# A hybrid attention and mLSTM layer on one core: head pairs on 64 rows each of TensorE, and two output units interleaved

## The reference

```python
# branch a: for each token, 128 keys are chosen by an index score; attention over them
s_idx = einsum('bthd,bsd->bths', qi, ki) * 64 ** -0.5        # 16 index heads of 64
score = einsum('bth,bths->bts', wi, relu(s_idx))             # masked by chunks of 64 tokens
_, idx = top_k(score, 128)
logits = einsum('bthd,btjhd->bthj', q, k[idx]) * 64 ** -0.5  # 8 heads of 64
out = einsum('bthj,btjhd->bthd', softmax(logits), v[idx])
# branch b: mLSTM with 4 heads of 128, gated and normalised by head
# merge
merged = sigmoid(g_a) * ((o_a * silu(a_z)) @ w_branch_a) + sigmoid(g_b) * (h_b @ w_branch_b)
y = rmsnorm(x + merged @ w_out) * final_norm_g
```

## Time and profile before

| | |
|---|---|
| median of 3 runs | 515.43 us |
| the profiled execution | 515.22 us, its span 513.5 us |
| PE matmuls busy | 503.4 us, 98%, 2506 of them |
| PE weight loads busy | 422.1 us, 82% |
| DVE, ACT, POOL busy | 252.1, 236.3, 214.0 us |
| DMA | 48.94 MB, 95 GB/s in the mean |

### The profile page before, as it was taken

How to read it: one execution, slowest core, us unless ns; L and a number is a source line. 1 busy time by engine, 2 the same in 40 slices (tenths; PEclk the granted TensorE clock), 3 DMA queues, 4 the chain that set the end, 5 groups by cost and what they waited for, 6 DMA issues and landing times.

```text
span 513.5 us, 6778 instructions
## 1 busy us (share of the span) xinstructions
PE 503.4 (98%) x2506; PEld 422.1 (82%) x2506; DVE 252.1 (49%) x564; ACT 236.3 (46%) x417; POOL 214.0 (42%) x142
## 2 busy tenths in 40 slices
PE   7999999999999999999999999999999999999995
PEld 7688888888888878788888888888888888887885
DVE  3875778877999915515645556311110011125333
ACT  6756754655534344455567643233321333152322
POOL 1675231333353442356486343056335653372000
PEclk9999999999999999999999999999999999999999
DMA  8744531222233422122213111142244426443112
GB/s 281 207 132 121 142 99 47 83 83 70 63 114 87 139 83 82 42 60 66 82 41 84 42 43 41 42 123 66 60 122 123 110 57 202 124 155 133 41 48 77
DMA packets 44841, 48.94 MB, mean 95 GB/s; under 512 B 4996, under 2 KB 29700, under 8 KB 44808
## 3 DMA queue, kind: packets, MB, share of 16 engines
q1 hardware_dynamic: 43944, 47.39, 31.4%
q10 hardware_dynamic: 864, 1.12, 0.6%
HBM read 46.40 MB, written 2.11 MB: 94 GB/s over the span
## 4 chain that ended last, share of the span: by engine, by line
PE 91%; DMA 3%; POOL 3%; issue 1%; ACT 1%; SPq 1%; DVE 0%; POOLq 0%; DVEq 0%; ACTq 0%
PE pj L1397 23%; PE pj L1398 22%; PE pj L1399 22%; PE ob L1504 3%; DMA w_raw<-in_w_in 2%; POOL w_lo L510 2%; PE tr L1498 2%; PE ob L1478 2%; PE qb L1468 2%; PE qb L1463 2%; PE qb L1462 2%; PE ob L1398 1%; PE qb L1398 1%; PE qb L1397 1%; PE ob L1397 1%; PE ob L1399 1%
## 5 line engine op out<-in xcount | busy, mean ns | idle before, releaser
L510 POOL TENSOR_TENSOR w_lo<-w_raw,w_hi 128x1024 fp32r<-128x1024 f32 x70 | 168.3, 2415 | 147.1 <-ACT w_hi L851 147.0
L1397 PE MATMUL pj<-w_hi,h_hi 128*128 128x512 f32 x272 | 112.8, 415 | 0.0
L1399 PE MATMUL pj<-w_hi,h_lo 128*128 128x512 f32 x272 | 106.5, 392 | 0.0
L1398 PE MATMUL pj<-w_lo,h_hi 128*128 128x512 f32 x272 | 106.5, 392 | 0.0
L1397 PE MATMUL pj<-h_hi,w_hi 128*128 128x512 f32 (+1 forms) x200 | 78.1, 390 | 1.0 <-DVE h_lo L1076 1.0
L851 ACT ACTIVATE w_hi<-w_raw 128x1024 fp32r<-128x1024 f32 (+1 forms) x72 | 73.5, 1045 | 9.6 <-DMA w_raw<-in_w_out 6.0
L1399 PE MATMUL pj<-h_hi,w_lo 128*128 128x512 f32 (+1 forms) x200 | 77.9, 389 | 0.0
L1398 PE MATMUL pj<-h_lo,w_hi 128*128 128x512 f32 (+1 forms) x200 | 77.9, 389 | 0.0
L1399 PEld LDWEIGHTS pj<-w_hi,h_lo 128*128 128x128 f32 x272 | 51.1, 188 | 11.4
L1397 PEld LDWEIGHTS pj<-w_hi,h_hi 128*128 128x128 f32 x272 | 51.2, 188 | 9.5 <-issue 1.0
L1398 PEld LDWEIGHTS pj<-w_lo,h_hi 128*128 128x128 f32 x272 | 51.3, 189 | 9.3 <-issue 1.0
(11 more groups left out here) (200 smaller groups left out, 828.8 us busy)
## 6 DMA issues: line engine op xcount, KB each, us to landing
w_raw<-in_w_in SPq DMA_DIRECT2D x60, 512.0 KB, 3.6
w_raw<-in_w_out SPq DMA_DIRECT2D x5, 512.0 KB, 3.6
x_tok<-in_x SPq DMA_DIRECT2D x4, 512.0 KB, 5.4
w_raw<-in_w_branch_a SPq DMA_DIRECT2D x8, 256.0 KB, 2.9
w_raw<-in_w_branch_b SPq DMA_DIRECT2D x8, 256.0 KB, 3.3
x_again<-in_x SPq DMA_DIRECT2D x1, 2048.0 KB, 9.0
w_late<-in_w_out SPq DMA_DIRECT2D x3, 512.0 KB, 7.2
neg_m_all<-neg_m_d SPq DMA_DIRECT2D x4, 256.0 KB, 5.0
```

The source lines that it names most:

```text
L510: eng.tensor_tensor(lo[:, 0:m], raw_slot(n)[:, 0:m], hi[:, 0:m].bitcast(F32), ALU.subtract).then_inc(lo_by_dve if n in DVE_SLOTS else lo_b ...
L1397: pe.matmul(bank, a_hi, b_hi, start=first, stop=False)
L1398: pe.matmul(bank, a_hi, b_lo, start=False, stop=False)
L1399: return pe.matmul(bank, a_lo, b_hi, start=False, stop=last)
```

## The change

Scores and logits are jobs of two heads each, `score` with 24 jobs instead of 48 and `qk_a` with 16 instead of 32. Head e of a pair has its features on rows 64e to 64e + 63, its queries and keys both, hi and lo in tiles of their own (`iq_parts[:, 0]` hi, `[:, 1]` lo; `k_parts` alike; `q_hi` and `q_lo` instead of `q_twice` and `q_lo`). Its three products go through `tile_position=(64 * e, 0)`, the two heads in turn, head e into bank `qb[e]`. A pair of scores stands where its first head stood; the pair of logits at the even places, while the softmax of one head (`soft`, a job that PE skips) stays at every place. A pair's job takes both banks of the ring. The splits of a whole unit are one copy and one subtraction over 128 rows. The first two output units run seven of their eight chunks each, then the last chunk of each. Of the last scaling ACT has 384 columns and DVE 640 (`SHARE`). Scores and logits are the three products hi by hi, hi by lo and lo by hi; before, the scores' two passes gave the fourth, lo by lo, as well.

```diff
-    for s in range(len(SCORES)):
-        put(score_place(s), "score", s)
+    for k in range(len(SCORES) // 2):
+        put(score_place(2 * k), "score", k)
...
         if p < len(ATTN):
-            put(q, "qk_a", p)
+            if p % 2 == 0:
+                put(q, "qk_a", p // 2)
+            put(q, "soft", p)
...
+        if job[0] in ("score", "qk_a"):
+            assert n[ring] % 2 == 0
+            before[job] = last.get((ring, 1))
+            last[(ring, 0)] = last[(ring, 1)] = job
+            continue
...
             elif kind == "score":
-                eng.wait_ge(relu_made, job[1] + 1)
+                eng.wait_ge(relu_made, 2 * job[1] + 2)
...
             elif kind == "qk_a":
-                eng.wait_ge(z_made, job[1] + 1)
+                eng.wait_ge(z_made, 2 * job[1] + 2)
...
-                    for e in range(2):
-                        src, hi, _ = part(job, e)
-                        act.activation(hi, src, ACT.Copy).then_inc(part_hi_made, 1)
+                    src, hi, _ = part(job)
+                    act.activation(hi, src, ACT.Copy).then_inc(part_hi_made, 1)
...
-                for e in range(2):
-                    same = slice(e * A_DIM, (e + 1) * A_DIM)
-                    act.activation(q_twice[same, i % 2, e, :, :], q_a[same, :, i * P:(i + 1) * P], ACT.Copy)\
-                        .then_inc(q_hi_made, 1)
-                for e in range(2):
-                    same, other = slice(e * A_DIM, (e + 1) * A_DIM), slice((1 - e) * A_DIM, (2 - e) * A_DIM)
-                    act.activation(q_twice[other, i % 2, e, :, :], q_a[same, :, i * P:(i + 1) * P], ACT.Copy)\
-                        .then_inc(q_doubled, 1)
+                act.activation(q_hi[:, i % 2, :, :], q_a[:, :, i * P:(i + 1) * P], ACT.Copy).then_inc(q_hi_made, 1)
...
-                    queries = iq_parts[:, h % 2, h // 2, (i - 1) * P:i * P]
-                    pe.matmul(bank[:, 0:w], queries, ik_hi[:, 0:w], start=True, stop=False)
-                    ins = pe.matmul(bank[:, 0:w], queries, ik_lo[:, 0:w], start=False, stop=True)
+                    for n, (part_q, keys) in enumerate(((0, ik_hi), (0, ik_lo), (1, ik_hi))):
+                        for e in range(2):
+                            same = slice(e * IDX_DIM, (e + 1) * IDX_DIM)
+                            ins = pe.matmul(bank[e][:, 0:w], iq_parts[same, part_q, h // 2, (i - 1) * P:i * P],
+                                            keys[same, 0:w], start=(n == 0), stop=(n == 2),
+                                            tile_position=(e * IDX_DIM, 0))
...
+                    for n, (part_q, part_k) in enumerate(((q_hi, 0), (q_hi, 1), (q_lo, 0))):
+                        for e in range(2):
+                            same = slice(e * A_DIM, (e + 1) * A_DIM)
+                            ins = pe.matmul(bank[e][:, 0:w], part_q[same, i % 2, b, :], k_parts[same, part_k, b, 0:w],
+                                            start=(n == 0), stop=(n == 2), tile_position=(e * A_DIM, 0))
...
-                    half = y_norm[:, i % 2, WIDTH:D_MODEL]
+                    half = y_norm[:, i % 2, SHARE:D_MODEL]
...
-            for m, (i, piece, cols) in enumerate(OUT_UNITS):
...
+            def out_part(m, ks):
...
+            for m in range(2):
+                out_part(m, range(KT - 1))
+            for m in range(2):
+                out_part(m, range(KT - 1, KT))
+            for m in range(2, len(OUT_UNITS)):
+                out_part(m, range(KT))
```

More of the change, by code:

```diff
@@ L726, in side @@
             def side(p):
-                if p == first_quarter("bo"):
-                    wait_full(pool, ("qk_b", B_HEADS - 1, TILES - 1))
-                    pool.wait_ge(lo_by_pool, sum(1 for m in range(group_slot("bz") + 1) if m not in DVE_SLOTS))
-                    for e in range(2):
-                        other = slice((1 - e) * A_DIM, (2 - e) * A_DIM)
-                        pool.memset(q_lo[other, :, e, :, :].bitcast(F32), 0.0).then_inc(q_lo_zeroed, 1)
-                        pool.wait_ge(q_lo_zeroed, e + 1)
                 if p in SPLIT_AT:
                     i = SPLIT_AT[p]
-                    for e in range(2):
-                        same = slice(e * A_DIM, (e + 1) * A_DIM)
[L739 to L743, removed]
+                    pool.wait_ge(q_hi_made, i + 1)
+                    pool.tensor_tensor(q_lo[:, i % 2, :, :], q_a[:, :, i * P:(i + 1) * P],
+                                       q_hi[:, i % 2, :, :].bitcast(F32), ALU.subtract).then_inc(q_lo_made, 1)
                 for job in SIDE.get(p, []):
@@ L796, in _ @@
                 if (g, j) == ("bq", 0):
-                    wait_full(pool, ("score", len(SCORES) - 1))
+                    wait_full(pool, ("score", len(SCORES) // 2 - 1))
                     pool.memset(v_b[:, :, :, B_DIM:B_DIM + 1], 1.0).then_inc(v_ones_made, 1)
@@ L886, in job_side @@
                     wait_full(act, job)
[L887 to L889 removed]
+                    src, hi, _ = part(job)
+                    act.activation(hi, src, ACT.Copy).then_inc(part_hi_made, 1)
                 elif kind == "score":
[L891 to L893 removed]
                     wait_full(act, job)
[L895 to L898, removed]
+                    for s in (2 * job[1], 2 * job[1] + 1):
+                        w = (SCORES[s][0] + 1) * P
+                        if s >= RELUS:
+                            act.wait_ge(relu_used, s - RELUS + 1)
+                        act.activation(ob[s % RELUS][:, 0:w], qb[s % 2][:, 0:w], ACT.Relu,
+                                       scale=float(IDX_DIM) ** -0.5).then_inc(relu_made, 1)
                 elif kind == "qk_b":
@@ L913, in job_side @@
                         .then_inc(cell_made, 1)
-                elif kind == "qk_a":
+                elif kind == "soft":
                     s = job[1]
@@ L1049, in _ @@
                     act.wait_ge(y_gained, m + 1)
-                    half = y_norm[:, i % 2, WIDTH:D_MODEL]
+                    half = y_norm[:, i % 2, SHARE:D_MODEL]
                     act.activation(half, half, ACT.Copy, scale=out_rstd[:, i:i + 1]).then_inc(y_scaled_act, 1)
                     act.wait_ge(y_scaled_act, i + 1)
-                    act.dma_start(out.rearrange("(t p) d -> p t d", p=P)[:, i, WIDTH:D_MODEL], half)\
+                    act.dma_start(out.rearrange("(t p) d -> p t d", p=P)[:, i, SHARE:D_MODEL], half)\
                         .then_inc(stored[i % 2], 16)
@@ L1421, in side @@
                 kind = job[0]
-                bank = bank_of(job)
+                if kind == "soft":
+                    return
+                bank = qb if kind in ("score", "qk_a") else bank_of(job)
                 if BEFORE[job] is not None:
@@ L1485, in side @@
                         wait_read(pe, ("stage_chan", len(STAGED) - 1))
-                        pe.wait_ge(q_lo_zeroed, 2)
                     if h == 0:
-                        pe.wait_ge(q_doubled, 2 * (i + 1))
-                        pe.wait_ge(q_lo_made, 2 * (i + 1))
-                    e, b = h % 2, h // 2
-                    pe.matmul(bank[:, 0:w], q_twice[:, i % 2, e, b, :], k_parts[:, e, b, 0:w], start=True, stop=False)
-                    ins = pe.matmul(bank[:, 0:w], q_lo[:, i % 2, e, b, :], k_parts[:, e, b, 0:w], start=False, stop=True)
+                        pe.wait_ge(q_lo_made, i + 1)
+                    b = h // 2
+                    for n, (part_q, part_k) in enumerate(((q_hi, 0), (q_hi, 1), (q_lo, 0))):
[3 more added lines that the diff above has]
+                                            start=(n == 0), stop=(n == 2), tile_position=(e * A_DIM, 0))
                 elif kind == "probs_chan":
```

59 lines of the change are left out of this document (28 added, 31 removed).

## The result

The changed kernel takes **523.22 us** (median of 4 runs, 523.11 to 523.47) against 515.38 for the kernel before (4 runs, 515.22 to 515.58): a ratio of 1.0153, interval 1.014 to 1.0166, slower by 7.8 us. The forecast was 527.9 in a range of 513.0 to 534.5, with 0.72 on slower: the direction and the range held, and the loss was put 4.7 us too high. The profiled execution took 523.11 us, its span 521.3, as against 515.22 and 513.5.

A forecast was written before the change was run, and what follows sets the result against it. PE (TensorE) was taken to bound the kernel, its matmuls busy for 98% of the span. 515.22 + 13.6 - 1.05 - 0.1 = 527.7 us in the profiled execution, 527.9 as a median; range 513 to 534.5.

The forecast's parts named there:

- Part 1: Score and logit pairs in three passes: each saves one period but pays two drains and open loads; together +13.6 us.
- rows 5: Profile rows at line 1444's eight transposes, the one row change before: about 0.11 us drain each way, loads 0.06 apart.
- p: Period of a pair's passes in the changed kernel: 0.228 us at 512 columns, 0.125 at 256 and 128.
- the middle case: Pairs' cost with the second half's load 0.06 us behind the first: +13.6 us, between ends +5.0 and +19.2.
- Part 2: Whole units split at once, saving DVE, ACT and POOL work that PE does not wait for: zero.
- Part 3: Waits for q banks that pairs fill: perhaps 0.4 us once at the first pair, costed at zero.
- Part 4: Output units reordered: 1.42 us wait for m_lo covered, 0.37 lost to a late bank read; net -1.05 us.
- Part 5: Shares of the last scaling: ACT from 512 to 384 columns, ACT's store being the later; -0.1 us.
- 1 (no cost of row change): Row-tiled loads go ahead while the full matmul streams, so row changes are free: 508.1 or 514.6 us; chance 0.28.
- 2 (loads one after another): The halves' loads come 0.11 us apart, one after another, with the drains: 533.5 us; chance 0.2.
- 3 (halves not together): The two halves of a pair do not run together, six periods a pair: +33, 547 us; chance 0.05.
- 4 (banks bind): Drains are nothing, but in half of 24 score pairs PE waits 0.8 us for ACT: 517.7 us; chance 0.05.

The follow-up runs named there:

- b_row64: The kernel before, with a matmul of 64 columns on rows 0 to 63 ahead of every second score and logit, 40 in all: 532.24 us, 1.0329.
- b_row128: Control: the kernel before with the same 40 small matmuls over all 128 rows: 519.93 us, 1.0092.
- b_col64: The kernel before with the same 40 small matmuls over all 128 rows, but with 64 weight columns: 519.64 us, 1.0087.
- a_same: The changed kernel with both heads of each pair on rows 0 to 63, odd heads computed from even heads' rows: 543.24 us, 1.0545 to the kernel before.
- b_out: The kernel before with only the changed order of the output units and SHARE 640: 513.96 us, 0.9977.
- b_share: The kernel before with only the last scaling and stores shared 640 to 384 (SHARE): 515.10 us, 0.9999.
- a_blocks: The changed kernel with a pair's three passes of head 0 written first, then the three of head 1: 523.44 us, 1.0159 to the kernel before.

## Why the prediction was right in direction and too high

**Part 1, the mechanism: right.** 24 + 16 pairs each save one period and pay two changes of rows with a load in the open, as rows 5 had shown for four rows and 32. b_row64 against b_row128 shows the row change, b_col64 that there is none for columns.

**Part 1, the size: the step that failed** is "the other half 0.06 behind, as the row-tiled loads in rows 5 stand". The halves' loads start together. The constant 0.49 of the forecast (T + 0.72 against T + 0.23) measured 0.41, 0.06 of the difference being this lag and the other 0.02 the gaps either side, 0.32 before the first load for 0.33 and 0.21 behind the last pass for 0.22. It counts 40 times: 3.2 us. The same step made p 0.125 at 256 and 128 columns, where loads side by side leave it at 0.115 and 0.11: 12 x 3 x 0.01 + 4 x 3 x 0.015 = 0.5 us. Together 3.7 of the 4.45 by which 13.6 exceeds the measured 5.80 + 3.35 = 9.15. The remaining 0.7 lies in the logits: 0.41 less a period would make 4.06 there, and the units with two pairs each grew on average by 0.46, 0.56, 0.37 and 0.29 for 128 to 512 columns, 3.35 in all. Quarters of units that hold the same transposes and products with the values, once with a logit or a pair and once without (every other place of the changed kernel), take it apart; us added to the quarter:

| columns | one logit before | two periods | a pair now | three periods + 0.41 |
|---|---|---|---|---|
| 128 | 0.226 | 0.22 | 0.68 | 0.74 |
| 256 | 0.24 | 0.23 | 0.75 | 0.755 |
| 384 | 0.357 | 0.34 | 0.92 | 0.92 |
| 512 | 0.46 | 0.456 | 1.09 | 1.094 |

So the logits before cost a little more than their periods (some 0.27 us over all 32), the pairs of 128 columns 0.06 less than the price (0.24 over four), and the four pairs that have the transposes of `gated` behind them another 0.05 less each. That is the 0.7. Why these two kinds of pair are cheaper was not tried.

Per score pair behind a full matmul, forecast and measured: +0.26 and +0.18 at 512 columns, +0.32 and +0.23 at 384 (medians of the starts), +0.41 and +0.29 at 256. In the forecast's own terms the measured 0.41 lies between its two readings of rows 5: 0.29 for the passage taken whole, the lower end of the range, and 0.49 for the middle case. The passage had transposes, whose loads last 0.14 us in this trace on 128 rows too, and not 0.19; that may be why it is the cheaper, which no run isolates. The 0.06 of the middle case was the wrong model for a plain reason: the eight transposes of line 1444 all read `a_row` and `nm_row`, rows 0 to 3, so their loads follow one another in the same group of 32 rows, and they say nothing of two halves on different rows. a_same shows the difference: with both halves on the same rows the first two loads start 0.11 us apart (46.51 and 46.62), in the changed kernel together (46.41).

The other terms nearly cancel: 0.43 for the start, which no forecast had, against 0.13 less from the output units and 0.17 from the shares.

**Part 2, zero: right.** 5.6 us of DVE, 14.0 of ACT and 7.2 of POOL went, and no stretch between the pairs moved: from unit 15 to the first logits both traces run level to 0.02 us.

**Part 3, the banks: zero was right,** and the one wait of 0.4 us that it allowed for did not come. The view puts the gap before the second pair's load to ACT's read, but that read was over before the full matmul ahead of the pair began; PE's matmuls, its weight loads, then ACT:

```profile
48.56 0.39 PE L1382 MATMUL pj<-w_hi,h_lo 128*128 128x512 f32 x1
...
48.88 0.18 PEld L1449 LDWEIGHTS qb<-ik_hi,iq_parts 64*128 64x128 f32 x2 [0.36 <-ACT ob L888]
...
47.42 1.07 ACT L888 ACTIVATE ob<-qb 128x512 f32<-128x512 f32 x2
```

ACT ends at 48.49, the load stands 0.32 behind the matmul's start, as at the first pair, and the score pairs of one width that stand behind a full matmul differ by less than 0.03 us among themselves. So the gap is the row change's and not the bank's. What a bank wait would add to a row change was not seen here.

**Part 4, -1.05: measured -0.92.** The wait for `m_lo` went whole. The new one, PE's timeline and then DVE's:

```profile
482.17 0.39 PE L1382 MATMUL pj<-w_hi,m_lo 128*128 128x512 f32 x1
482.76 0.50 PE L1380 MATMUL pj<-w_hi,m_hi 128*128 128x512 f32 x1 [0.20 <-DVE y_tok L1361]
483.10 0.40 PE L1381 MATMUL pj<-w_lo,m_hi 128*128 128x512 f32 x1
...
482.01 0.69 DVE L1361 TENSOR_TENSOR y_tok<-pj,x_again 128x512 f32<-128x512 f32 x1 [5.22 <-PE pj L1382]
```

483.10 stands where 482.62 would, two periods behind 482.17: 0.48 lost for the 0.37 forecast, since DVE's read began at T + 0.52 (T is 481.49) and not at T + 0.43. 1.42 - 0.48 = 0.94, which is what b_out shows.

**Part 5, -0.1: nothing that the times can tell, and +0.07 in the traces.** The scaling is 0.1 us shorter on ACT and 0.07 longer on DVE, as said. What was left out is the stores: SP's grew with DVE's share from 256 to 320 KB, and ACT's shrank to 192. The end of b_share, all engines, then ACT's store in the list of DMA issues (KB, us to landing) of the kernel before and of the changed one:

```profile
509.36 0.61 ACT L1052 ACTIVATE y_norm<-y_norm,out_rstd 128x384 f32<-128x384 f32 x1 [0.23 <-DVE out_rstd L1386]
509.36 0.55 DVE L1389 TENSOR_SCALAR y_norm<-y_norm,out_rstd 128x640 f32<-128x640 f32 x1
510.00 0.34 ACTq L1054 DMA_DIRECT2D out<-y_norm  x1
...
out<-y_norm ACTq DMA_DIRECT2D x1, 256.0 KB, 2.4
...
out<-y_norm ACTq DMA_DIRECT2D x1, 192.0 KB, 2.6
```

ACT's store is issued 0.1 us sooner than in rows 9, but takes 0.2 longer to land although it is smaller, and it lands last with either share. Behind the end of PE's last matmul the traces with the new shares take 5.29 to 5.30 us, those with the old 5.22 to 5.24. The median of b_share is that of the kernel before. That the larger store beside it is what delays it was not tried.

**The rivals.** 1 (no cost of row change) falls by b_row64. 2 (loads one after another) falls by the loads that start together. A load on 64 rows lasts 0.18 to 0.19 us, as one on 128 does. That is as the Trainium skill, page TensorE: Matmul & The Clock Gate, section LDWEIGHTS, has it; but two halves take it at once. 3 (halves not together) is what a_same brings about: 543.2, where it had said 547. 4 (banks bind) falls by the second pair and its like above.

## What to carry to other kernels

A pair of half-height tiles saves one pass and pays a fixed price for leaving the full array and coming back, here 0.41 us; between full matmuls two pairs of 512 columns at a stretch just reach it (2.01 to 2.03 us against 2.05), and by the same sum 256 columns need four, which no run tried. Before splitting the array, look for the one place in the profile where its height already changes, price the whole passage, and ask whether its tiles lie on the same rows or on different ones, as yours will. What a faster side engine saves is worth nothing while PE waits for none of it; and where a late operand stalls PE, put ahead as much as covers the delay and keep the rest for behind, since the other bank's reader needs cover too.

## What the runs showed that was not expected

- Matmuls on different rows started against the order of the program (a_blocks: the fourth ahead of the second, 10 ns behind the first).
- The loads of two halves ran side by side, 0.19 us each, and at 128 columns two matmuls a period of 0.11 went through.
- Changing the columns of a tile costs nothing that can be measured (40 changes there and back: 4.3 us against 4.6 for the same matmuls at full width), changing its rows 0.31 us.
- The view named ACT's read as what ended a gap of PE's loads, though the read had ended before the last full matmul began; only the times of both engines side by side showed it.
- Before the first score the same code ran up to 0.55 us shorter in one profiled execution than in another.
